# Two modulation pieces summed by TensorE, router weights built earlier, and norm rows spread on chip in a two-block network

## The reference, cut to what matters

```
mod = silu(c) @ ada_w[i] + ada_b[i]              # 6 x 1024 values
sh1, sc1, g1, sh2, sc2, g2 = split(mod)
h = x * (1 + sc1) + sh1
y = neighbourhood_mixer(h) if i == 0 else gqa_mixer(h)
x = layer_norm(ALPHA * x + (1 + g1) * y, ln_g[i, 0], ln_b[i, 0])
h = x * (1 + sc2) + sh2
y = hierarchical_moe(h)                          # router, 32 experts, 2 per token
x = layer_norm(ALPHA * x + (1 + g2) * y, ln_g[i, 1], ln_b[i, 1])
```

## Time and profile before

| | us |
|---|---|
| median of 3 runs | 1516.74 |
| lowest, highest | 1512.55, 1517.01 |
| the profiled execution's own time | 1517.6 |
| its span, first to last instruction | 1515.9 |
| PE busy | 1375.5 |
| DVE busy | 550.2 |
| ACT busy | 216.2 |
| POOL busy | 83.6 |

### The profile page before, as it was taken

One profiled execution on the slowest core, in us unless ns is written; L12 is line 12 of the kernel. 1 busy time (PEld: TensorE's weight loads), 2 busy tenths in 40 slices (PEclk: granted clock), 3 DMA queues, 4 the chain that ended last, 5 costly groups with the idle time before them and its releaser, 6 DMA issues.

```text
span 1515.9 us, 28729 instructions
## 1 busy us (share of the span) xinstructions
PE 1375.5 (91%) x12954; PEld 876.6 (58%) x12954; DVE 550.2 (36%) x1263; ACT 216.2 (14%) x574; POOL 83.6 (6%) x91
## 2 busy tenths in 40 slices
PE   8999999999999999879879799889999797797796
PEld 4886488578886556436445354467665363353453
DVE  3696669665853221111111106584211111111113
ACT  3230123022332000000000002442000000000000
POOL 3100111000003000000000001100200000000000
PEclk9999999999999999889889899999999899898998
DMA  9657955778869999999999998328999999999995
GB/s 347 234 198 258 335 193 197 285 268 305 308 268 395 416 427 425 427 427 427 428 426 426 428 398 325 111 112 337 424 410 425 427 426 427 426 425 428 426 422 219
DMA packets 94742, 531.20 MB, mean 350 GB/s; under 512 B 5248, under 2 KB 7488, under 8 KB 70800
## 3 DMA queue, kind: packets, MB, share of 16 engines
q1 hardware_dynamic: 91456, 519.40, 84.7%
q0 software_dynamic: 3152, 9.86, 1.8%
HBM read 528.19 MB, written 1.05 MB: 349 GB/s over the span
## 4 chain that ended last, share of the span: by engine, by line
PE 61%; DMA 27%; DVE 8%; SPq 1%; ACT 1%; issue 1%; DVEq 0%; ACTq 0%
PE bk L458 23%; DMA ring<-in_moe_w_down 17%; PE bk L965 17%; DMA AR<-in_moe_w_down 9%; PE bk L999 8%; PE bk L1044 4%; DVE mpart L1142 3%; PE bk L531 3%; PE bk L454 2%; PE bk L709 1%; DVE AR L1134 1%; PE bk L724 1%; SPq L2538 1%; ACT AR L2019 1%; PE bk L680 1%
## 5 line engine op out<-in xcount | busy, mean ns | idle before, releaser
L965 PE MATMUL bk<-ring,AR 128*32 128x128 f32 x4480 | 267.3, 409 | 3.4 <-DMA ring<-in_moe_w_up 3.1
L1134 DVE TENSOR_TENSOR AR<-bk,AR 128x128 f32<-128x128 f32 (+2 forms) x106 | 41.3, 389 | 516.2 <-ACT AR L2019 450.7
L965 PEld LDWEIGHTS bk<-ring,AR 128*32 128x32 f32 x4480 | 176.1, 128 | 85.9 <-DMA ring<-in_moe_w_up 5.2
L965 PE MATMUL bk<-AR 128*32 128x128 f32 x3712 | 222.9, 409 | 2.4 <-DMA AR<-in_moe_w_up 2.0
L2019 ACT ACTIVATE AR<-bk 128x512 f32<-128x512 f32 (+4 forms) x182 | 75.1, 435 | 932.0 <-PE bk L965 757.6
L965 PEld LDWEIGHTS bk<-AR 128*32 128x32 f32 x3712 | 145.3, 127 | 72.7 <-DVE X L1134 4.5
L999 PE MATMUL bk<-ring,AR 128*32 128x512 f32 x544 | 139.1, 708 | 42.4 <-DMA ring<-in_moe_w_down 42.4
L458 PE MATMUL bk<-AR,ring 128*128 128x256 f32 (+1 forms) x832 | 170.7, 364 | 1.6 <-DVE diag L1134 1.6
L458 PE MATMUL bk<-ring,AR 128*128 128x256 f32 (+1 forms) x608 | 159.8, 421 | 1.8 <-DVE diag L1134 1.1
L458 PEld LDWEIGHTS bk<-AR,ring 128*128 128x128 f32 x832 | 147.6, 191 | 21.2 <-issue 3.5
L999 PE MATMUL bk<-AR 128*32 128x512 f32 x352 | 131.6, 714 | 27.7 <-DMA AR<-in_moe_w_down 27.7
(11 more groups left out here) (174 smaller groups left out, 980.8 us busy)
## 6 DMA issues: line engine op xcount, KB each, us to landing
ring<-in_moe_w_gate SPq DMA_DIRECT2D x36, 2048.0 KB, 28.8
ring<-in_moe_w_up SPq DMA_DIRECT2D x34, 2048.0 KB, 26.4
AR<-in_moe_w_up SPq DMA_DIRECT2D x30, 2048.0 KB, 29.0
ring<-in_moe_w_down SPq DMA_DIRECT2D x30, 2048.0 KB, 33.9
AR<-in_moe_w_gate SPq DMA_DIRECT2D x28, 2048.0 KB, 26.7
AR<-in_moe_w_down SPq DMA_DIRECT2D x26, 2048.0 KB, 33.9
ring<-in_ada_w SPq DMA_DIRECT2D x24, 2048.0 KB, 11.0
ring<-in_w_in SPq DMA_DIRECT2D x11, 2048.0 KB, 15.2
```

The source lines that it names most:

```text
L965: ins = eng.matmul(o[32 * f:32 * f + 32, 128 * m:128 * m + 128], XG[u][:, c, 32 * j:32 * j + 32], w[:, c, f::4], start=c == 0, stop=c == N ...
L1134: return eng.tensor_tensor(o, a, b, op)
```

## The change

Three edits, and one due time that changes with them.

- The last two modulation pieces, 22 and 23, are no longer summed by DVE. `direct_total(11, ...)` multiplies them on PE by `CCB`, in which each column of `ccol` stands 32 times: 8 chunks by 4 column parts, 32 matmuls. It stands as filler in round 4 of the grouped attention (`"direct"`). `extract(11)` moves from the first expert group of layer 1 to the side work of round 5 (`"x11"`), and `total(11, 6)` goes from `output`.
- In layer 1, `norm_columns(2, ...)` and `router_weights(1)` move from rounds 6 and 7 of the attention to the place behind the rotation of the first key tile; their scratch moves from `diag` to the arena. `CCB` is written there too.
- The rows of the first norm of both layers come as 4 KB DMAs to one partition. PE and ACT spread them behind the third expert (`j == 2`) of the first group, through banks 5 and 6; `finish` waits for all four copies.

```diff
-GQA_ROUNDS = (("q01",), ("r10",), ("q11",), ("r01",), (), ("r11",), ("o00",), ("l", "o01"), ("o02",), ("o03",))
-GQA_SIDE = (("v10",), ("w10",), ("v01", "w01"), (), ("v11", "+", "w11"), ("+",), ("n", "+"), ("m", "+", "o00"), ("l", "o01"),
-            ("o02", "o03", "s"))
-GQA_LOADS = (..., ("ada", 22, 70), ("ada", 23, 85))
+GQA_ROUNDS = (("q01",), ("r10",), ("q11",), ("r01",), ("direct",), ("r11",), ("o00",), ("l", "o01"), ("o02",), ("o03",))
+GQA_SIDE = (("v10",), ("w10",), ("v01", "w01"), (), ("v11", "w11"), ("x11",), (), ("o00",), ("l", "o01"), ("o02", "o03", "s"))
+GQA_LOADS = (..., ("ada", 22, 70), ("ada", 23, 71))
...
+            def direct_total(m, b):
+                o = begin(b, "adaT", m)
+                pe.wait_ge(sem("ccb"), 1)
+                for g in range(2):
+                    pe.wait_ge(*loaded("ada", 2 * m + g))
+                for c in range(NC):
+                    for g in range(4):
+                        w = piece(("ada", 2 * m + g // 2), NC, 512)[:, c, 256 * (g % 2):256 * (g % 2) + 256]
+                        ins = eng.matmul(o[32 * g:32 * g + 32, 0:256], CCB[:, c, :], w, start=c == 0, stop=c == NC - 1)
+                end(ins, "adaT", m)
+                for g in range(2):
+                    DONE["ada", 2 * m + g] = filled("adaT", m)
...
-                total(10 + i, 6)
+                if not i:
+                    total(10, 6)
...
-            def norm_row(k, w, dst):
+            def norm_row(k, w, dst, to):
                 for h in range(2):
-                    o = begin((3, 5 if w else 4)[h], "row", k, w, h)
+                    o = begin(to[h], "row", k, w, h)
...
                         if j:
                             hidden(j - 1)
+                        if not q and j == 2:
+                            norm_row(2 * i, 0, LN_IN[0], (5, 6))
+                            norm_row(2 * i, 1, LN_IN[1], (5, 6))
...
             def router_weights(i):
-                if i:
-                    for h in range(2):
-                        v.wait_ge(*filled("g1", 1, h))
...
                 for f in ROPED[0:3]:
                     variance(f)
                     rotate(f)
+                    if f == "k0":
+                        v.tell(eng.tensor_copy(CCB, bcast(ccol[:, 0:NC], 2, 32)), sem("ccb"), 1)
+                        norm_columns(2, 1, 3, "comb", 2)
+                        router_weights(1)
...
-                            extract(10 + i)
+                            if not i:
+                                extract(10)
...
+                        if not q and j == 2:
+                            norm_row(2 * i, 0, LN_IN[0])
+                            norm_row(2 * i, 1, LN_IN[1])
...
-                norm_row(2 * i, 1, LN_IN[1])
+                small(LN_IN[1][0:1, :], A["ln_b"][i, 0:1, :], f"row{2 * i}1")
                 g.wait_ge(sem("raw"), 2 * i + 2)
-                norm_row(2 * i, 0, LN_IN[0])
+                small(LN_IN[0][0:1, :], A["ln_g"][i, 0:1, :], f"row{2 * i}0")
...
-                g.wait_ge(sem(f"row{2 * i}"), 32)
+                for n in range(2):
+                    for h in range(2):
+                        g.wait_ge(*drained("row", 2 * i, n, h))
```

More of the change, by code:

```diff
@@ L79 @@
             ("wo", 0, 498), ("wo", 1, 505))
[L80 to L83 removed]
+GQA_ROUNDS = (("q01",), ("r10",), ("q11",), ("r01",), ("direct",), ("r11",), ("o00",), ("l", "o01"), ("o02",), ("o03",))
+GQA_SIDE = (("v10",), ("w10",), ("v01", "w01"), (), ("v11", "w11"), ("x11",), (), ("o00",), ("l", "o01"), ("o02", "o03", "s"))
+GQA_LOADS = ((2, 14), (0, 39), (1, 52), ("wo", 0, 115), ("wo", 1, 123), ("ada", 22, 70), ("ada", 23, 71))
 ROPED = ("k0", "k1", "q00", "q10", "q01", "q11")
@@ L249, in program @@
         COMB = cst[:, K_S1 + 64:K_S1 + 112].rearrange("p (n w c) -> p n w c", n=3, w=2)
+        CCB = cst[:, K_S1 + 112:K_S1 + 368].rearrange("p (c k) -> p c k", c=NC)
         bn_s = st[:, 0:24].rearrange("p (t c n) -> p t c n", t=NT, c=2)
@@ L277, in rt @@
             return view(A_ROWS + 2560 + o, *dims)
-        LTMP = diag[:, 0:288].rearrange("p (c n) -> p c n", c=NC)
-        LPART = diag[:, 288:360]
+        LTMP = diag[:, 0:288].rearrange("p (c n) -> p c n", c=NC), view(8192, NC, 36)
+        LPART = diag[:, 288:360], view(8480, 72)
         R_L, R_ASG, R_PM = rt(0, NT, 36), rt(256, NT, 32), view(A_AG + 512, NT, 32)
@@ L517, in router_sums @@
                 pe.wait_ge(sem("lpart"), i + 1)
-                end(product(o[:, 0:72], [(ones[:, :], LPART)]), "lsum", i)
+                end(product(o[:, 0:72], [(ones[:, :], LPART[i])]), "lsum", i)
             def first_layer(l):
@@ L878, in fill @@
                     for f in todo.pop(0):
-                        if f == "l":
+                        if f == "direct":
+                            direct_total(11, next_bank())
+                        elif f == "l":
                             router_sums(1, next_bank())
@@ L1047, in experts @@
                     if q == NQ - 1:
-                        norm_row(2 * i + 1, 0, LN_OUT[0])
+                        norm_row(2 * i + 1, 0, LN_OUT[0], (3, 4))
                         o = down_rows()
@@ L1054, in experts @@
                         end_sums(sums)
-                        norm_row(2 * i + 1, 1, LN_OUT[1])
+                        norm_row(2 * i + 1, 1, LN_OUT[1], (3, 5))
                     else:
@@ L1552, in router_weights @@
                     v.chain()
-                    v.step(tt(LTMP, wr[:, i, :, :], bcast(COMB[:, 2 * i, w, :], 2, 36), ALU.mult))
+                    v.step(tt(LTMP[i], wr[:, i, :, :], bcast(COMB[:, 2 * i, w, :], 2, 36), ALU.mult))
                     v.chain()
-                    ins = red(LPART[:, 36 * w:36 * w + 36], LTMP.rearrange("p c n -> p n c"), ALU.add)
+                    ins = red(LPART[i][:, 36 * w:36 * w + 36], LTMP[i].rearrange("p c n -> p n c"), ALU.add)
                     if w:
@@ L2286, in settle @@
                     for f in todo.pop(0):
-                        if f[0] not in "tlo":
+                        if f[0] not in "dtlo":
                             take(f)
@@ L2402, in layer_loads @@
                 small(sgw, A["sg_w"][l], f"lay{l}")
-            def norm_row(k, n, dst):
-                small(dst, A[("ln_g", "ln_b")[n]][k // 2, k % 2:k % 2 + 1, :].to_broadcast([P, D]), f"row{k}")
             def norm_before(i):
                 g.wait_ge(*drained("o", TAG[i], 7))
-                norm_row(2 * i, 1, LN_IN[1])
+                small(LN_IN[1][0:1, :], A["ln_b"][i, 0:1, :], f"row{2 * i}1")
                 g.wait_ge(sem("raw"), 2 * i + 2)
-                norm_row(2 * i, 0, LN_IN[0])
+                small(LN_IN[0][0:1, :], A["ln_g"][i, 0:1, :], f"row{2 * i}0")
             def norm_after(i):
```

## The result

| | before | after |
|---|---|---|
| median of the runs, us | 1515.93 (5 runs, 1512.55 to 1517.01) | 1524.11 (5 runs, 1523.74 to 1527.61) |
| profiled execution, its own time | 1517.6 | 1523.74 |
| span | 1515.9 | 1522.0 |

The ratio after to before is 1.0056, with an interval of 1.0043 to 1.0069: 8.2 us slower by the medians, 6.1 us by the profiled executions. The median of 1524.11 lies inside the stated range of 1513 to 1525, but 3.4 us above the sum (1520.7) and outside the 1519 to 1523 that the forecast gave as its own. As a difference the forecast had 4.0 us and the runs show about twice that. By the bound of 0.3% it counts as slower, which had the chance 0.41; "same" had 0.47.

What follows compares the result with a forecast made beforehand. TensorE's release of slots in each layer's first expert group, plus fixed bytes, was taken as the bound. Layer 0 +4.5 and layer 1 +3.5 - 4.0 made +4.0 on 1517.6, so 1521.6, or 1520.7 us at the median; range 1513 to 1525.

Steps and rivals of the forecast that it cites:

- What bounds it: First expert group, both layers: TensorE sets when slots free for the next loads; the layer's end is that release plus bytes.
- Norm rows on TensorE: Behind group 0's third expert: eight instructions cost 3.5 us a layer, plus 1.0 us waiting for bank 6 in layer 0.
- Bytes worth 0: Norm-row broadcasts on POOL's queue: removing them gains 0, though they took 2.75 us of all DMA engines per layer.
- The first rival: DMA transfers set the pace at the releases, hiding the norm rows: faster, 1510.7 us at the median; chance 0.13.
- `finish`: POOL, first expert group: starts near 499.9, ends near 510.7 us, just in time for ACT's gather copies; cost 0.
- Direct sum on TensorE: Round 4 of the grouped attention: 32 matmuls take 3.8 us, in the gap that was there.
- The attention's gain: Layer 1's grouped attention: 4.0 us earlier, from a 2.2 us shorter chain to group 6's scores and 1.7 us of clock.
- the full clock for scores and output quarter: Group 6's scores and the output quarter: idle falling to 1.75 us keeps TensorE's clock full, worth 1.7 us.
- DVE's later relief: Attention from the next output quarter on: TensorE has the work, so relieving DVE there is worth nothing.
- Router weights at 0: DVE behind layer 1's first keys: 3.3 us of moved work cost 0, or 0.5 with cover gone.
- the second rival: Attention gives little, clock falls all the same: gain 1 us, 1523.7 us; chance 0.17 together with a zero-gain variant.
- the slow rivals: Attention gaining 1 us or nothing (1523.7, 1524.7 us; 0.17 together), or `finish` late by 2 us per layer (1524.7; 0.05).

Runs made afterwards that it cites:

- bank7: Changed kernel with the second halves of the norm rows in bank 7 instead of bank 6; 1521.02 us, ratio 1.0025 to before.
- early2_full: attn_only plus 4 KB norm rows, loaded earlier, spread by 128-row products replacing unused router products, `finish` held behind first expert's gate and up; 1515.77 us, ratio 0.9991.
- attn_only: Changed kernel with only the attention edits, norm rows by 512 KB broadcasts as before; 1515.02 us, ratio 0.9989 to before.
- direct_only: attn_only without the earlier router weights and norm columns, so only the direct sum is changed; 1515.03 us, ratio 0.9983 to before.
- weights_only: Kernel before with only layer 1's norm columns and router sums moved behind the first keys; 1517.24 us, ratio 0.9997.
- rows_only: Changed kernel with only the norm-row edits, the attention as before; 1528.03 us, ratio 1.0073 to before.
- early2_k1: early2_full with one-row products instead of 128-row products for the norm rows; 1524.37 us, ratio 1.0051 to before.
- pair: bank7 with the two halves of each norm row on different array rows, to run side by side; 1522.92 us, ratio 1.0038 to before.
- late_full: bank7 with each norm row spread by a 128-row product instead of a one-row product; 1522.79 us, ratio 1.0034 to before.

## Why the prediction was right or wrong, step by step

- **What bounds it: right.** "The release, plus bytes" held to 0.1 us in layer 1 (412.8 and 412.9 us from release to end), and the DMA engines ran dry about 4 us ahead of both releases, as the longer dry stretch in the list of signs asked. The releases came at 519.18 us (forecast 519.5) and 1109.15 (near 1107).
- **Norm rows on TensorE: right, a little low.** 3.5 us a layer forecast, 3.7 to 3.8 measured (`bank7`). The row that the forecast read gives this: 1.9 us for four instructions are 0.48 each, so 3.8 for eight; the 0.44 of the prediction stands in no row of it. The wait for bank 6 in layer 0 was 0.8 us of idle at the place forecast; with it and the half clock in the last instructions layer 0 pays 5.4 instead of 4.5, layer 1 3.85 instead of 3.5. Together 9.2 us where 8.0 stood.
- **Bytes worth 0: right** (`early2_full`, and the idle DMA ahead of the releases in after). The first rival, with 0.13, is refuted.
- **`finish`: right.** It began at 499.74 (forecast 499.9), ended at 510.4 (510.7), and took 5.97 and 4.66 us. ACT waited for it and nobody waited for ACT. That POOL would be stretched did not happen.
- **Direct sum on TensorE: right,** 3.66 us against 3.8, in the gap.
- **The attention's gain: the step that failed.** 4.0 us forecast, 2.2 in the traces between the same marks, 1.7 by `attn_only`'s ratio and 2.6 by `direct_only`'s. Of its two terms the chain's was right, 1.9 for 2.2. The other, "the full clock for scores and output quarter, worth 1.7 us", was wrong: the scores gained 0.86, the output quarter lost 0.92. The argument that an idle time of 1.75 us would not drop the clock fell: behind 1.92 or 1.93 us all nine kernels with the direct sum have the output quarter at 4.9 to 5.4 us, while `weights_only` and `rows_only` kept the full clock behind 1.43 and 1.63. So one of the forecast's own signs, no clock at 0.50 in rounds 5 and 6, did not come. It also read one execution's placing of the low clock as a fact of the schedule: `rows_only` had it elsewhere, and gained only 0.2 us by it. The remaining 0.3 us of the 2.2 are the wait for DVE at 1010.43 us, 0.23 us in before and gone in after; the prediction had put DVE's later relief at nothing.
- **Router weights at 0: right beside the direct sum** (`direct_only` does without them and is no slower than `attn_only`). By themselves they remove a wait for DVE that was 0.23 us in before's trace and 1.67 in that of `rows_only`.
- **The sum.** With measured sizes, 9.2 less 2.2 is 7.0 us, against 8.2 measured by the medians and 6.1 in the profiled executions, whose start of layer 0 and whose clock differ by 1 to 2 us in places without an edit. The forecast of 4.0 was low by 1.8 us in the attention and by 1.2 us in the rows. The measured median is 0.4 us above the second rival's 1523.7, and the clock falling all the same is that rival's mechanism. That the range held is owed to the room it left for the slow rivals and not to the sum.

A row that was in the trace and was not read could have been a warning: the existing norm row. Stretches of the kernel before, behind the row at 899.65:

```profile
901.00:903.00 2.00, 2.00 (x10) 0.37 (x12) 0.00 (x0) 1.01 (x2) 0.00 (x0) 0.70 1.04 393
903.00:905.00 2.00, 2.00 (x24) 1.08 (x20) 0.00 (x0) 0.00 (x0) 0.00 (x0) 0.50 0.86 333
```

The clock falls behind one-row products there as well. TensorE had waited 0.74 and 0.52 us shortly ahead of them, so this row alone doesn't tell which of the two did it.

## What to carry to other kernels

A transfer that is not the last to end is worth nothing, however large; before trading bytes for instructions, look whether the DMA engines run dry ahead of the release that the stage waits for, and price the instructions in full if they stand on the engine that sets the release. If they must be there, stand them where that engine waits anyway (`early2_full`: 3.85 us for nothing) rather than in a gapless row of work (3.7 to 3.8 us each time). Before a slow clock is counted as a gain to be had, look at what ends next to last behind it. Read gains of an edit between two marks around it, and keep apart what the granted clock did, which can change from one execution to the next: several traces with the same order tell what repeats.

The best version run is `direct_only` (0.9983, 0.9975 to 0.9992), with `attn_only` and `early2_full` not to be told from it.

## What was not expected of the hardware

- **One-row products let the granted clock fall while TensorE is busy.** Behind eight of them, back to back in 3.7 to 4.0 us, it went from 1.00 to 0.50 in both layers of `bank7`, in layer 1 of after and in layer 0 of `early2_k1`; in `rows_only`, `pair` and layer 0 of after waits of 0.8 to 1.2 us stood among them too. Behind the same amount over 128 rows it stayed at 1.00 in both layers of `late_full` and in layer 0 of `early2_full`. The rule of the Trainium skill (TensorE: Matmul & The Clock Gate, What's actually happening) ties the clock to how busy TensorE has been; by the busy time of the profile these cases are equal, so that measure alone doesn't tell them apart. Why one row and 128 differ is not shown.
- **The low clock's price depends on what runs.** Products of 128x128 in four column parts took the same at both levels; a gather of 32 products on the full array took 5.64 us instead of 3.81, and 6.32 in layer 1 of `early2_k1`.
- **Small DVE operations with two SBUF inputs took about 1.9 us each beside POOL's,** 0.19 without it.
- **Two one-row products on different rows of the array ran side by side,** four instructions in 1.13 us, the time of two.
